# Products of constants in TensorE's order at the norms of a two-block transformer kernel

## The chip, the cores and the metric

The kernel runs on one core of a Trainium2 chip. The metric is the device time of one execution in microseconds (us). Three runs of the kernel before gave 3358.14, 3357.20 and 3356.77 us, median 3357.2.

## The reference

One sequence of 512 tokens of width 1024 goes through three transformer layers: two of a first block (the first one also carries 256 context tokens) and one of a second block. Each layer is

```python
x = x + 0.5 * m[2] * swiglu(modulate(x, g0, m[0], m[1]), wi1, wo1)
x = x + m[5] * mixer(modulate(x, g1, m[3], m[4]))
x = x + 0.5 * m[8] * swiglu(modulate(x, g2, m[6], m[7]), wi2, wo2)
```

with `modulate(z, g, shift, scale) = rmsnorm(z, g) * (1.0 + scale) + shift`, where `rmsnorm` divides each token by the root of the mean of its squares. The mixer is window attention beside gated linear attention in the first layer, a pooling mixer in the second, and mLSTM beside dilated attention in the third. After the first block, and again at the end, stands `rmsnorm(x, final_g)`. All inputs are float32. So there are eleven norms on the way: three in each layer, one between the blocks, one at the end.

## The kernel before

The state `XT` lies in SBUF with features on the 128 partitions, in eight blocks `k` of 128 features by 512 tokens (768 with the context). A program of `Step` objects is written in one order; each engine then walks that order and emits its own part of every step, so the order of the steps is the order of each engine's queue. Each engine waits by semaphores.

Dense products keep fp32 accuracy by splitting: a weight and an activation each become a rounded high part (`WH`, `HH`) and a low rest (`WL`, `HL`), and `dense` (L197 to L202) issues three products of 512 columns for each block of 128 by 128. Small products, the norms' sums and spreads among them, take plain fp32 operands. The program issues such a call once, and the trace shows it as two MATMUL instructions: 48 calls at L489 stand there as 96.

A norm has these parts, on four engines:

- While the stage before still adds its results to `XT`, ScalarE squares each block and VectorE adds the squares into `SA` (`Sums`, L418).
- `RstdSum` (L474): TensorE waits for the last addition, then sums `SA` over the partitions, one call of 128 columns for each 128 tokens (L489, four calls, six with the context). VectorE and ScalarE then compute the factor, one over the root, in six short operations (`Newton`, L463 to L471).
- `RstdSpread` (L501): TensorE waits for the factor, then spreads it over all partitions into banks 4 and 5 (L513, as many calls).
- `NormSplit` (L543): VectorE multiplies a block by the factor (L581), ScalarE rounds it with the shift into `HH` (L562), VectorE takes the rest into `HL` (L570). TensorE's first dense product waits for the first block's `HL`. In `Up` of the first chunk (`c == 0`) the 48 products go block by block, six for each of the eight blocks.

`rstd_of` (L2941) adds the sum and the spread. It is called by `norm_split` for every feed-forward and for both attention mixers, by `mixer_pool`, and by `final_norm` (L2995), that is at ten of the eleven norms; the first norm, in `start`, has its own order. `final_norm` ends in `FinalNorm` (L588), which multiplies the eight blocks of `XT` on VectorE (L612); between the two blocks it also collects the next norm's squares, and TensorE has nothing to do in it. `P.K` holds constants: its columns 0 to 127 are ones, and 128 to 255, `P.ID`, are the identity. Bank 3 belongs to the first products of a feed-forward and is empty at these places.

Of the kernel before, what the change touches and what calls it, by code (L numbers as in the profile page):

```python
# [17 lines left out]
T = 512  # L18
# [28 lines left out]
NONE = Tok(None, 0)  # L47


class Sig:  # L50


    def __init__(self, sem):
        self.sem, self.n = sem, 0
# [18 lines left out]
class Step:  # L73
# [3 lines left out]
    def tensor(self, pe):  # L77
        pass
# [4 lines left out]
    def vector(self, dve):  # L83
        pass
# [364 lines left out]
class Newton:  # L449
# [11 lines left out]
    def vector(self, dve, R, V, ss, width):  # L461
        dve.wait_ge(*self.ready)
        dve.e.tensor_scalar(V, ss, 1.0 / width, EPS, ALU.mult, ALU.add).then_inc(self.v.sem, 1)  # L463
        dve.wait_ge(*self.root)
        dve.e.reciprocal(R, R).then_inc(self.inv.sem, 1)
        dve.wait_ge(*self.inv)
        dve.e.scalar_tensor_tensor(V, V, -0.5, R, ALU.mult, ALU.mult).then_inc(self.half.sem, 1)
        dve.wait_ge(*self.half)
        dve.e.tensor_tensor(V, V, R, ALU.mult).then_inc(self.prod.sem, 1)
        dve.wait_ge(*self.prod)  # L470
        dve.e.scalar_tensor_tensor(R, V, 1.5, R, ALU.add, ALU.mult).then_inc(self.done.sem, 1)  # L471


class RstdSum(Step):  # L474
# [2291 lines left out]
class Program:  # L2766
# [171 lines left out]
            self.add(ModDone(self, 0, 1, 2, dot))  # L2938
            return [muled, dot]

    def rstd_of(self, nq):  # L2941
        self.add(RstdSum(self, nq))
        self.add(RstdSpread(self, nq))

    def norm_tiles(self, ctx, two):
        sb = lambda n, s: self.sb(ctx, self.name(n), s, F32R)
        return H(sb("HH", [128, 8, T]), sb("HL", [128, 8, T]), sb("HC", [128, 8, 2 * TC]) if two else None)
# [45 lines left out]
        self.spread = step.done  # L2993

    def final_norm(self, gname, again):  # L2995
        self.rstd_of(T // 128)
        self.add(FinalNorm(self, gname, Sums(self, T) if again else None))

# [700 lines left out]
```

## Time and profile before

| | |
|---|---|
| median of three runs | 3357.2 us |
| profiled execution | 3361.52 us, of which 3359.7 us span |
| TensorE busy, matmul | 3120.8 us, 93% |
| VectorE busy | 1905.1 us, 57% |
| ScalarE busy | 1024.9 us, 31% |
| mean granted TensorE clock | 0.955 of full speed |

One execution was recorded. Times in its rows are microseconds from the start of the span unless marked ns. PE is TensorE's matmul, PEld its weight load, DVE VectorE, ACT ScalarE. A matmul's duration contains the way through the array, so that matmuls overlap; what one costs in a stream is the distance of its start to the next one's. PEclk is the granted clock as a share of 2.4 GHz; it has two levels here, 1.00 and 0.50 (1.2 GHz).

### The profile page before, as it was taken

Reading aid. Unit: us, or ns where it says so; the run is one execution under the profiler, and the core shown is the slowest. Engines: PE = TensorE matmul, PEld = TensorE weight load, DVE = VectorE, ACT = ScalarE, POOL = GpSimd, SP = SyncE. Lnnn points to the kernel's source line nnn. Section 1 sums busy time; section 2 is a strip of 40 time slices with the busy share of each in tenths; the row PEclk is TensorE's granted clock in tenths of the full one; section 3 lists DMA queues with packets and bytes.
Section 4 is the critical chain, followed back from the end, with each engine's and each line's share of the span. In section 5 each row is a group of like instructions: output and inputs, shape, how many; then the busy total and the mean of one; then the engine's idle time right before and its main releaser. Section 6 shows DMA issues by size and latency. Waiting matters only on the chain.

```text
span 3359.7 us, 36404 instructions
## 1 busy us (share of the span) xinstructions
PE 3120.8 (93%) x14707; PEld 2504.8 (75%) x14718; DVE 1905.1 (57%) x2717; ACT 1024.9 (31%) x1476; POOL 28.0 (1%) x30
## 2 busy tenths in 40 slices
PE   4999999898889999999997999979998998899998
PEld 3788888786667888778876788768887764577886
DVE  6876555635555544566656654566665555654344
ACT  2322222335433222322224222332223434432222
POOL 2000000000000000000000000000000000000000
PEclk6999999998999999999997999989999999799999
DMA  5433332110023433255531443225551210122321
GB/s 192 132 128 129 125 113 97 52 63 16 1 95 112 161 126 121 82 188 187 189 114 63 157 144 132 94 82 188 194 194 54 82 57 1 49 90 94 100 95 50
DMA packets 101794, 364.98 MB, mean 109 GB/s; under 512 B 11198, under 2 KB 12494, under 8 KB 101372
## 3 DMA queue, kind: packets, MB, share of 16 engines
q1 hardware_dynamic: 97644, 351.65, 31.2%
q10 hardware_dynamic: 2944, 6.29, 0.5%
q0 software_dynamic: 1040, 4.71, 0.4%
q8 instruction: 118, 1.93, 0.2%
q14 instruction: 48, 0.39, 0.0%
HBM read 360.51 MB, written 2.10 MB: 108 GB/s over the span
## 4 chain that ended last, share of the span: by engine, by line
PE 85%; DVE 9%; ACT 3%; issue 1%; DMA 1%; ACTq 0%; POOL 0%; DVEq 0%; SPq 0%; POOLq 0%
PE ps L197 24%; PE ps L199 24%; PE ps L198 24%; PE ps L201 4%; PE ps L202 2%; DVE WL L189 1%; DVE DUMP L310 1%; DMA STG<-in_w_modt 1%; ACT WH L184 1%; DVE RAW L1278 1%; PE ps L513 1%; PE ps L2563 1%; PE ps L2323 1%; PE ps L2633 0%; PE ps L2663 0%
## 5 line engine op out<-in xcount | busy, mean ns | idle before, releaser
L197 PE MATMUL ps<-HH,WH 128*128 128x512 f32 x2464 | 979.9, 398 | 35.0 <-DVE HL L570 28.4
L199 PE MATMUL ps<-HH,WL 128*128 128x512 f32 x2464 | 967.6, 393 | 0.0
L198 PE MATMUL ps<-HL,WH 128*128 128x512 f32 x2464 | 967.5, 393 | 0.0
L184 ACT ACTIVATE WH<-RAW 128x1024 fp32r<-128x1024 f32 x456 | 456.9, 1047 | 554.7 <-PE ps L199 410.1
L189 DVE TENSOR_TENSOR WL<-RAW,WH 128x1024 fp32r<-128x1024 f32 x456 | 538.5, 1221 | 85.6 <-ACT WH L184 85.4
L197 PEld LDWEIGHTS ps<-HH,WH 128*128 128x128 f32 x2464 | 468.0, 190 | 142.7 <-issue 40.8
L198 PEld LDWEIGHTS ps<-HL,WH 128*128 128x128 f32 x2464 | 468.3, 190 | 100.2 <-issue 4.6
L199 PEld LDWEIGHTS ps<-HH,WL 128*128 128x128 f32 x2464 | 467.5, 190 | 99.8
L821 DVE SCALAR_TENSOR_TENSOR XT<-ps,DER,XT 128x512 f32<-128x512 f32 x512 | 342.8, 682 | 272.3 <-PE ps L199 257.8
L197 PE MATMUL ps<-GH,WH 128*128 128x512 f32 x1056 | 414.2, 392 | 19.1 <-DVE XT L821 14.3
L762 DVE TENSOR_TENSOR S<-S,ps 128x512 f32<-128x512 f32 x132 | 90.8, 688 | 568.1 <-PE ps L199 568.1
L198 PE MATMUL ps<-GL,WH 128*128 128x512 f32 x1056 | 411.9, 390 | 0.0
L199 PE MATMUL ps<-GH,WL 128*128 128x512 f32 x1056 | 411.6, 390 | 0.0
L744 ACT ACTIVATE GH<-S 128x512 fp32r<-128x512 f32 x132 | 83.4, 632 | 670.6 <-DVE S L762 670.6
L310 DVE SCALAR_TENSOR_TENSOR DUMP<-RAW,CC 128x1024 bf16<-128x1024 f32 x200 | 244.4, 1222 | 11.6 <-DVE DUMP L310 0.5
L197 PEld LDWEIGHTS ps<-GH,WH 128*128 128x128 f32 x1056 | 198.8, 188 | 67.1 <-DVE XT L821 18.6
L199 PEld LDWEIGHTS ps<-GH,WL 128*128 128x128 f32 x1056 | 198.8, 188 | 42.2
L198 PEld LDWEIGHTS ps<-GL,WH 128*128 128x128 f32 x1056 | 198.9, 188 | 38.5
L740 ACT ACTIVATE S<-ps 128x512 f32<-128x512 f32 x132 | 79.0, 598 | 293.2 <-PE ps L199 293.2
L201 PE MATMUL ps<-HC,WH 128*128 128x512 f32 x424 | 151.8, 398 | 0.0
L764 DVE TENSOR_TENSOR GL<-S,GH 128x512 fp32r<-128x512 f32 x132 | 91.4, 692 | 100.3 <-ACT GH L744 100.3
L202 PE MATMUL ps<-HC,WL 128*128 128x256 f32 x424 | 118.8, 280 | 0.0
(355 smaller groups left out, 2424.9 us busy)
## 6 DMA issues: line engine op xcount, KB each, us to landing
RAW<-in_w_modt SPq DMA_DIRECT2D x200, 512.0 KB, 4.5
RAW<-in_ffn_wi SPq DMA_DIRECT2D x176, 512.0 KB, 4.4
RAW<-in_ffn_wo SPq DMA_DIRECT2D x88, 512.0 KB, 4.7
RAW<-in_w_gu SPq DMA_DIRECT2D x88, 512.0 KB, 4.3
RAW<-in_w_in SPq DMA_DIRECT2D x44, 512.0 KB, 3.7
RAW<-in_w_down SPq DMA_DIRECT2D x44, 512.0 KB, 4.5
RAW<-in_w_out SPq DMA_DIRECT2D x16, 512.0 KB, 4.5
MU<-in_w_mod SPq DMA_DIRECT2D x8, 384.0 KB, 9.0
```

The lines of the kernel that those rows point to most:

```text
L184: act.e.activation(u.hi, u.ld.view, ACT.Copy).then_inc(u.hi_done.sem, 1)
L189: dve.e.tensor_tensor(u.lo, u.ld.view, u.hi.bitcast(F32), ALU.subtract).then_inc(u.lo_done.sem, 1)
L197: pe.e.matmul(out, wh, x[0], start=first, stop=False)
L198: pe.e.matmul(out, wh, x[1], start=False, stop=False)
L199: m = pe.e.matmul(out, wl, x[0], start=False, stop=last)
L201: pe.e.matmul(out, wh, x, start=first, stop=True, skip_group_check=not first)
L202: m = pe.e.matmul(out[:, 0:TC], wl, x[:, 0:TC], start=False, stop=True, skip_group_check=True)
L310: dve.e.scalar_tensor_tensor(self.dump, self.view, 1.0, tile[:, :], ALU.mult, ALU.mult, accum_out=self.P.DOT[:, self.row % 2, j, self.f:se ...
L744: act.e.activation(gh, s, ACT.Copy).then_inc(self.hi[n].sem, 1)
L762: dve.e.tensor_tensor(s, s, F.SX[:, :] if n else out, ALU.mult).then_inc(self.mul[n].sem, 1)
L764: dve.e.tensor_tensor(gl, s, gh.bitcast(F32), ALU.subtract).then_inc(self.lo[n].sem, 1)
L821: dve.e.scalar_tensor_tensor(x, o, P.mod_g(F.mi, d, j), x, ALU.mult, ALU.add).then_inc(self.evac[d, n][i].sem, 1)
```

## The change

A new step `Busy(n)` puts `n` fp32 calls into TensorE's order, each with the identity as the stationary operand and 256 columns of the constants moving, written to bank 3, where nobody reads them. At nine norms eight calls stand ahead of the sums, twelve between the sums and the spread, and ten behind the spread. At the last norm only the eight stand. In the final norm between the blocks, a further `Busy(4)` follows each of the first seven blocks, with a wait for that block. Nothing else changes: no other engine gets a new instruction.

```diff
--- before.py
+++ after.py
@@ -469,6 +469,19 @@
         dve.e.tensor_tensor(V, V, R, ALU.mult).then_inc(self.prod.sem, 1)
         dve.wait_ge(*self.prod)
         dve.e.scalar_tensor_tensor(R, V, 1.5, R, ALU.add, ALU.mult).then_inc(self.done.sem, 1)
+
+
+class Busy(Step):
+
+
+    def __init__(self, P, n, after=NONE):
+        self.P, self.n, self.after = P, n, after
+
+    def tensor(self, pe):
+        P = self.P
+        pe.wait_ge(*self.after)
+        for _ in range(self.n):
+            pe.e.matmul(P.banks[3][:, 0:256], P.ID, P.K[:, 0:256], start=True, stop=True)
 
 
 class RstdSum(Step):
@@ -2938,9 +2951,15 @@
             self.add(ModDone(self, 0, 1, 2, dot))
             return [muled, dot]
 
-    def rstd_of(self, nq):
+    def rstd_of(self, nq, last=False):
+        self.add(Busy(self, 8))
         self.add(RstdSum(self, nq))
+        if last:
+            self.add(RstdSpread(self, nq))
+            return
+        self.add(Busy(self, 12))
         self.add(RstdSpread(self, nq))
+        self.add(Busy(self, 10))
 
     def norm_tiles(self, ctx, two):
         sb = lambda n, s: self.sb(ctx, self.name(n), s, F32R)
@@ -2993,8 +3012,11 @@
         self.spread = step.done
 
     def final_norm(self, gname, again):
-        self.rstd_of(T // 128)
-        self.add(FinalNorm(self, gname, Sums(self, T) if again else None))
+        self.rstd_of(T // 128, last=not again)
+        final = self.add(FinalNorm(self, gname, Sums(self, T) if again else None))
+        if again:
+            for k in range(7):
+                self.add(Busy(self, 4, final.done[k]))
```

## Rows read from the trace of the kernel before

**Rows 1.** The page: the chain that ended last, by engine.

```profile
PE 85%; DVE 9%; ACT 3%; issue 1%; DMA 1%; ACTq 0%; POOL 0%; DVEq 0%; SPq 0%; POOLq 0%
```

**Rows 2.** TensorE by line: count, busy us, mean ns, idle before.

```profile
L197 PE MATMUL ps<-HH,WH 128*128 128x512 f32 x2464 | 979.9, 398 | 35.0 <-DVE HL L570 28.4 <-DVE WL L189 5.1 <-ACT S L740 1.2
...
L489 PE MATMUL ps<-SA,K 128*6 128x128 f32 x96 | 16.9, 338 | 60.6 <-DVE SA L418 31.6 <-POOL SA L446 29.0
```

**Rows 3.** Timeline, TensorE at one norm: start us, us, line, tiles, count, idle before.

```profile
1002.23 0.39 PE L199 MATMUL ps<-MH,WL 128*128 128x512 f32 x1
1004.86 1.04 PE L489 MATMUL ps<-SA,K 128*6 128x128 f32 x8 [2.24 <-DVE SA L418]
1008.52 2.07 PE L513 MATMUL ps<-R,SEL 6*128 6x128 f32 x8 [2.63 <-DVE R L471]
1013.13 0.76 PE L197 MATMUL ps<-HH,WH 128*128 128x512 f32 x1 [2.54 <-DVE HL L570]
```

**Rows 4.** Stretches around that norm: busy by engine, then PEclk, DMA share, GB/s.

```profile
1002.62:1005.62 3.00, 0.76 (x7) 0.62 (x8) 2.04 (x3) 2.12 (x3) 0.00 (x0) 1.00 0.81 295
1006.00:1016.00 10.00, 4.94 (x15) 4.09 (x16) 7.06 (x13) 3.09 (x5) 0.00 (x0) 0.50 0.00 0
```

**Rows 5.** Timeline, TensorE in the pool mixer: products of 256 and of 140 columns.

```profile
1777.41 0.28 PE L1108 MATMUL ps<-WPH,HH 128*128 128x256 f32 x1
1777.53 0.28 PE L1109 MATMUL ps<-WPH,HL 128*128 128x256 f32 x1
...
1779.56 2.07 PE L1146 MATMUL ps<-BAND,Z 128*128 128x136 f32 x16
```

**Rows 6.** Timeline, TensorE near the start: fp32 products of 512 columns.

```profile
12.05 3.76 PE L266 MATMUL ps<-CC,K 128*128 128x512 f32 x4
15.60 2.05 PE L266 MATMUL ps<-CX,K 128*128 128x512 f32 x4
```

**Rows 7.** Timeline, TensorE: dense products at full clock, then one fp32 call.

```profile
1016.40 0.39 PE L199 MATMUL ps<-HH,WL 128*128 128x512 f32 x1
...
1025.24 0.39 PE L199 MATMUL ps<-HH,WL 128*128 128x512 f32 x1
1025.47 1.02 PE L266 MATMUL ps<-CC,K 128*128 128x512 f32 x2
...
1026.56 0.40 PE L198 MATMUL ps<-HL,WH 128*128 128x512 f32 x1
```

**Rows 8.** Stretches from a norm's first product to the 49th, three of six.

```profile
1013.13:1025.47 12.34, 12.34 (x48) 10.11 (x49) 12.03 (x16) 8.01 (x10) 0.00 (x0) 0.88 0.00 0
1390.82:1403.72 12.90, 12.90 (x49) 10.49 (x50) 12.51 (x16) 8.01 (x10) 0.00 (x0) 0.84 0.04 4
...
2205.27:2218.82 13.55, 13.55 (x48) 10.99 (x49) 12.50 (x16) 8.00 (x10) 0.00 (x0) 0.80 0.06 13
```

**Rows 9.** Timeline, TensorE at the norm ahead of the hybrid mixer.

```profile
2575.88 1.86 PE L489 MATMUL ps<-SA,K 128*6 128x128 f32 x8 [2.24 <-DVE SA L418]
```

**Rows 10.** Timeline, TensorE at the norm of the first mixer, with six column blocks.

```profile
642.19 0.28 PE L202 MATMUL ps<-GC,WL 128*128 128x256 f32 x1
645.49 1.48 PE L489 MATMUL ps<-SA,K 128*6 128x128 f32 x12 [3.02 <-DVE SA L418]
650.64 2.79 PE L513 MATMUL ps<-R,SEL 6*128 6x128 f32 x12 [3.67 <-DVE R L471]
655.97 0.76 PE L197 MATMUL ps<-HH,WH 128*128 128x512 f32 x1 [2.53 <-DVE HL L570]
```

**Rows 11.** Timeline, TensorE: the first product of the pool mixer.

```profile
1770.99 0.55 PE L1108 MATMUL ps<-WPH,HH 128*128 128x256 f32 x1 [4.48 <-DVE HL L570]
```

**Rows 12.** Timeline, TensorE from the final norm between the blocks on.

```profile
2184.11 2.07 PE L513 MATMUL ps<-R,SEL 6*128 6x128 f32 x8 [2.63 <-DVE R L471]
2196.17 1.87 PE L489 MATMUL ps<-SA,K 128*6 128x128 f32 x8 [9.98 <-DVE SA L418]
...
2205.27 0.77 PE L197 MATMUL ps<-HH,WH 128*128 128x512 f32 x1 [2.53 <-DVE HL L570]
```

## The prediction

> **What bounds the kernel now.** I read the chain of work that ended last first: 85% of it is TensorE [rows 1], and the table beside it says that TensorE is busy for 93% of the span. So whatever is put into TensorE's order is free only where TensorE waits, and only for as long as it waits. Next come TensorE's groups by line, for the waits: the norms' sums stood after 60.6 us of idle time, the first products behind a norm after most of 28.4 us [rows 2]. Then one norm in order of time [rows 3]: the last dense product starts at 1002.23, the sums at 1004.86, the spread at 1008.52, the first dense product at 1013.13. The three gaps are 2.24, 2.63 and 2.54 us. Last, the granted clock there [rows 4]: it is 1.00 after the last product, and 0.50 (1.2 GHz) from before 1006.0 to 1016.0, with TensorE busy for only 4.94 of these 10 us. The spread and the first dense products run at half speed. That is what can be won: not the waits, which belong to VectorE and ScalarE, but the slow work between them.
>
> **The price of one added call.** No call of this very form is in the trace. The program's fp32 call is two instructions in the trace, as the count at L489 shows. Between dense products at full clock, one such call of 512 columns stands from 1025.47 to 1026.56 together with one dense product [rows 7]. Dense products are 0.227 apart (39 steps from 1016.40 to 1025.24), so the call took 0.86 us, and 256 columns would take 0.43. From below, sixteen fp32 instructions of about 140 columns, weights of 128 by 128 as here, take 2.07 us with the last one's way through the array, about 0.12 each [rows 5], so the weight load does not show even there. From above, a dense product of 512 columns in one pass takes 0.227, twice that is 0.453. I take 0.43 us, because [rows 7] is the same operation at twice the width, with 0.427 and 0.453 as bounds; at the lower clock it is 0.86. Eight calls are then 3.44 us, twelve 5.16, ten 4.30, four 1.72. The first three are each longer than the gap that they stand in.
>
> Dense products of 256 columns are only 0.12 apart [rows 5]; by that pace a call of two instructions would be 0.24 us. The Trainium skill says much the same (TensorE: Matmul & The Clock Gate, Back-to-back issue gap: a matmul of 256 columns every 262 cycles at full clock, 0.11 us). The skill also says that true fp32 takes four passes (FP8 and Floating Point Precision, TensorE Precision Notes), with which the 0.86 us agrees. By the first figure the change would win time, about the sum of the first rival below, which is worked out from the row.
>
> **One ordinary norm, step by step** (at 1002) [rows 3].
> - Ahead of the sums: the last product holds TensorE to 1002.46, eight calls to 1005.90, against 1004.86: **+1.04**.
> - Ahead of the spread: the four calls of the sums hold TensorE for about 0.88 (eight instructions, 0.11 apart, from their 1.04 us), then twelve calls: the spread starts 6.04 after the sums, where the factor let it start after 3.66: **+2.38**. The factor itself is ready on time; the spread is queued behind the calls.
> - Behind the spread: at full clock it occupies 0.88 too, then ten calls, so the first product comes 5.18 after the spread's start. Before it was 4.61 (2.07 of slow spread, then 2.54 of the first block on VectorE and ScalarE, whose HL the first product waits for). **+0.57**. The 1.0 us that the fast spread wins is inside this.
> - So the first dense product comes 3.99 us late. Then it is repaid: the 48 products of the first chunk took 12.34 us at a mean clock of 0.88 [rows 8]; at full clock they are 48 x 0.227 = 10.88. Before, they would have had to wait for VectorE's blocks at that pace; now the blocks are ahead, since TensorE comes 3 us after them. **-1.46**. Net **+2.5**.
>
> **The other norms.** The stretch of 48 products exists at six norms, from 12.34 to 13.55 us, together 78.13, so 12.85 us are won back in all six [rows 8].
> - The norm at 1382: the same 3.99, less 2.02: +2.0.
> - At 2576 and 2968 the sums themselves were slow, 1.86 us instead of 1.04 [rows 9], because the clock fell ahead of them. The calls keep it up: 3.99 - 0.83 = 3.16 late, less 2.28 and 2.23: +0.9 each.
> - At 1801, behind the pool mixer, the clock is low already when the eight calls begin, and they cost up to 0.86 each until it rises. I estimate +1.6 ahead of the sums (1.0 to 3.5), then as at 2576: +1.5.
> - At 645, with six column blocks, the last product is a short one and the wait is 3.02 [rows 10]: 642.31 + 3.44 = 645.75, +0.26; 12 x 0.11 + 5.16 = 6.48 against 5.15, +1.33; 1.32 + 4.30 = 5.62 against 5.33, +0.29. 1.9 late. The slow clock lasts there to 661, 5.1 us from the first product, of which 2.4 come back: -0.5.
> - Ahead of the pool mixer, TensorE waits 4.48 us behind the spread, since VectorE first splits the pool weights [rows 11]. The lateness is 2.0 at the first product and its slow products run six us; I take 0, between -0.8 and +0.8.
> - The last norm has only the eight calls: +1.04, and perhaps a faster spread, whose cold 2.07 would be 1.05: +0.5.
>
> **The norm between the blocks** is the largest term [rows 12]. Before, TensorE has one wait of 9.98 us there while VectorE scales eight blocks. Now 10 + 7 x 4 + 8 = 46 calls stand between the spread and the next sums, 19.8 us, and the waits on blocks do not matter, as VectorE's pace is about 1.3 us a block and four calls take 1.72. The first spread starts at 2184.11 + 1.04 + 2.38 = 2187.53; with 0.88 + 19.78 the next sums start at 2208.19, against 2196.17: +12.0. Then +6.04 and +5.18: the first product at 2219.41 against 2205.27, 14.1 late. 2.67 come back: **+11.5**.
>
> **The sum:** 2.5 + 2.0 + 0.9 + 0.9 + 1.5 - 0.5 + 0 + 0.5 + 11.5 = **+19.3 us**. On the profiled execution of 3361.5 that is 3380.8; the median of the runs lies 4.3 lower, so 3357.2 + 19.3 = **3376.5**. The stages behind the norms are TensorE's own, so nothing there takes the lateness back. With 0.427 and 0.453 for a call (some 270 calls lie on the path) the sum is 18.5 to 25, the estimated terms add 3 either way.
>
> **The rivals.**
> 1. *A call costs 0.24 us*, two dense instructions of 256 columns. Then 1.92 and 2.40 us fit into the waits of 2.4 and 3.57 (the last with the spread), 2.88 misses by 0.1, and four calls (0.96) fit between the blocks. Each norm wins the 1.0 of the spread and some 1.2 to 2.4 behind it, the four slow sums 0.8 each: -24, **3333**. Against it stands [rows 7]. The sign turns at about 0.34 us a call: there eight calls cost +0.3, twelve +1.3, ten win 0.35, and repayment covers the rest.
> 2. *The calls do not keep the clock up.* They are made of ones and zeros. Then a call is 0.86 us: eight cost +4.5, twelve with a slow sum and spread +8.1, ten +5.8, nothing is repaid, 18 a norm; with the 46 calls the sum is near +175, **3530**. Against it: products with a diagonal matrix, nearly all zeros, ran four in 3.76 us at the start, and the next four in 2.05 [rows 6]; the clock rose on them.
> 3. *The lateness is taken back later*: TensorE finds weights and banks further ahead than now, which saves it the 5.1 us of waits on `WL` and some at chunk borders [rows 2]. Then +9: **3366**.
>
> **How the numbers follow.** Forecast 0.80, rival 1 0.07, rival 2 0.04, rival 3 0.09. The likeliest gives 3376.5. Its own bounds are 3372 to 3385; to take in rival 3 and an error in the estimated terms I give **3365 to 3389**. A measurement of this kernel can tell about 0.2% (6.7 us) from no change. Faster 0.07 (rival 1), within 0.2% 0.05 (part of rival 3), slower 0.88.
>
> **What would show it.** TensorE's groups get 2 x 306 = 612 instructions at the new line, 0.21 to 0.23 us apart. The waits at L489, L513 and at the first L197 behind a norm vanish from TensorE; the spreads take 1.05 instead of 2.07; the granted clock stays 1.00 through every norm, its mean near 0.99. The sums stand 1.0 us later after the last product, the spread 6.0 after the sums, the first product 5.2 after the spread. Between 2187 and 2208 TensorE is full while VectorE waits. Starts 3.7 us after the sums and a first product 3.6 after the spread would show rival 1; a clock of 0.50 in the new calls rival 2.

## The result and the profile after

The changed kernel takes 3384.6 us (median of four runs, 3379.2 to 3385.1) against 3357.5 us for the kernel before. The ratio is 1.0077, with a 95% interval of 1.0065 to 1.0089, so it is slower by 27 us (22 to 30). The profiled execution has 3385.1 us and a span of 3383.3 us, 23.6 us more than the span before.

The page of the changed kernel: busy time, the granted clock in 40 slices, and the chain that ended last.

```profile
PE 3224.4 (95%) x15330; PEld 2597.4 (77%) x15330; DVE 1904.4 (56%) x2717; ACT 1024.8 (30%) x1476; POOL 27.9 (1%) x30
...
PEclk6999999998999999999999999999999999799999
...
PE 88%; DVE 7%; ACT 3%; issue 1%; DMA 1%; ACTq 0%; DVEq 0%; SPq 0%
```

TensorE is busy 103.6 us more and its share of the chain grew from 85% to 88% [rows 1]. The mean granted clock rose from 0.955 to 0.973. More clock and more time together: what the clock gave is less than what the new calls took.

TensorE's groups by line and shape. The sums are now L502, the spreads L526, the new calls L484.

```profile
L197 PE MATMUL ps<-HH,WH 128*128 128x512 f32 x2464 | 973.6, 395 | 17.6 <-DVE HL L583 10.2 <-DVE WL L189 6.6 <-ACT S L753 0.4
...
L484 PE MATMUL ps<-K 128*128 128x256 f32 x612 | 139.3, 384 | 0.0
...
L526 PE MATMUL ps<-R,SEL 6*128 6x128 f32 x96 | 14.9, 301 | 6.0 <-DVE R L471 6.0
L502 PE MATMUL ps<-SA,K 128*6 128x128 f32 x96 | 13.6, 291 | 29.9 <-POOL SA L446 29.9
```

The waits that the change aimed at are gone. The idle time ahead of the sums was 60.6 us and is 29.9, all of it at the kernel's start; that ahead of the first products fell from 28.4 to 10.2, of which the first norm, which has no new calls, holds nearly everything [rows 2]. The 96 instructions of the spreads take 14.9 us where they took 23.9:

```profile
L513 PE MATMUL ps<-R,SEL 6*128 6x128 f32 x96 | 23.9, 426 | 30.7 <-DVE R L471 30.7
```

One norm in order of time, the one shown as [rows 3].

```profile
1002.44 0.39 PE L199 MATMUL ps<-MH,WL 128*128 128x512 f32 x1
1002.67 3.61 PE L484 MATMUL ps<-K 128*128 128x256 f32 x16
1006.21 1.04 PE L502 MATMUL ps<-SA,K 128*6 128x128 f32 x8
1007.18 5.45 PE L484 MATMUL ps<-K 128*128 128x256 f32 x24
1012.56 1.15 PE L526 MATMUL ps<-R,SEL 6*128 6x128 f32 x8
1013.64 4.58 PE L484 MATMUL ps<-K 128*128 128x256 f32 x20
1017.88 0.58 PE L197 MATMUL ps<-HH,WH 128*128 128x512 f32 x1
```

No row has an idle time any more. Eight calls stand from 1002.67 to 1006.21, 0.44 us each. The sums start 3.77 us behind the last dense product's start instead of 2.63, the spread 6.35 behind the sums instead of 3.66, the first product 5.32 behind the spread instead of 4.61: 4.5 us late.

Four stretches, with PEclk third from the end: the one that was at 0.50 before [rows 4], the first 48 products [rows 8], the stretch in which the calls behind the pool mixer begin (at 1804.03), and the norm between the blocks.

```profile
1006.00:1016.00 10.00, 10.00 (x53) 8.16 (x52) 4.11 (x8) 1.65 (x3) 0.00 (x0) 1.00 0.01 4
1017.88:1028.80 10.92, 10.92 (x50) 9.02 (x49) 10.65 (x14) 7.10 (x9) 0.00 (x0) 1.00 0.00 0
1802.50:1805.75 3.25, 3.25 (x13) 2.89 (x13) 3.25 (x6) 1.60 (x3) 0.00 (x0) 0.50 0.76 255
2187.00:2208.00 21.00, 21.00 (x103) 17.75 (x103) 13.01 (x22) 7.52 (x13) 0.00 (x0) 1.00 0.00 1
```

In the first, TensorE is busy all the time and the clock stays at 1.00 (it was 0.50, with 4.94 of 10 us busy). In the second, the 48 products run at full clock. From the first start to the last they take 10.9 us where they took 12.1; up to the start of the product behind them, as [rows 8] counts, 11.1 instead of 12.34. In the third the clock was low before the calls began, and rose behind 3.25 us of busy TensorE; these eight calls take 4.5 us and not 3.5. In the fourth TensorE is full for 21 us with new calls and one group each of sums and spreads, while VectorE, which has the real work there, is busy for 13.

The norm between the blocks, in the place of [rows 12].

```profile
2195.86 1.15 PE L526 MATMUL ps<-R,SEL 6*128 6x128 f32 x8
2196.95 20.12 PE L484 MATMUL ps<-K 128*128 128x256 f32 x92
2217.00 1.04 PE L502 MATMUL ps<-SA,K 128*6 128x128 f32 x8
...
2223.35 1.15 PE L526 MATMUL ps<-R,SEL 6*128 6x128 f32 x8
...
2228.66 0.58 PE L197 MATMUL ps<-HH,WH 128*128 128x512 f32 x1
```

The span of 23.6 us can be put down place by place, from the last product of one norm to that of the next, each against the same stretch of the kernel before:

| norm near (before) | forecast | measured |
|---|---|---|
| 645 | -0.5 | -0.1 |
| 1005 | +2.5 | +3.3 |
| 1383 | +2.0 | +2.8 |
| 1761, pool mixer | 0 | 0.0 |
| 1801 | +1.5 | +1.7 |
| 2180 and 2196 | +11.5 | +13.0 |
| 2576 | +0.9 | +0.7 |
| 2968 | +0.9 | +1.7 |
| the last | +0.5 | +0.2 |
| ahead of all | 0 | +0.3 |

### The profile page after: what moved, and what is told of

Same layout as the page of the kernel before. It is cut to its first block, busy times and chain, and to the rows that moved or that the text cites. A ratio compares the mean times of both kernels' runs of the same rounds, so it can differ in the third digit from the quotient of the medians.

```text
span 3383.3 us, 37639 instructions
## 1 busy us (share of the span) xinstructions
PE 3224.4 (95%) x15330; PEld 2597.4 (77%) x15330; DVE 1904.4 (56%) x2717; ACT 1024.8 (30%) x1476; POOL 27.9 (1%) x30
## 3 DMA queue, kind: packets, MB, share of 16 engines
q8 instruction: 123, 2.02, 0.2%
## 4 chain that ended last, share of the span: by engine, by line
PE 88%; DVE 7%; ACT 3%; issue 1%; DMA 1%; ACTq 0%; DVEq 0%; SPq 0%
PE ps L197 24%; PE ps L199 23%; PE ps L198 23%; PE ps L484 4%; PE ps L201 4%; PE ps L202 2%; DVE WL L189 1%; DVE DUMP L310 1%; DMA STG<-in_w_modt 1%; ACT WH L184 1%; DVE RAW L1291 1%; PE ps L2576 1%; PE ps L2676 1%; PE ps L2336 1%; PE ps L2646 0%
## 5 line engine op out<-in xcount | busy, mean ns | idle before, releaser
L197 PE MATMUL ps<-HH,WH 128*128 128x512 f32 x2464 | 973.6, 395 | 17.6 <-DVE HL L583 10.2
L484 PE MATMUL ps<-K 128*128 128x256 f32 x612 | 139.3, 384 | 0.0
```

Of the source, the lines that this page charges most:

```text
L197: pe.e.matmul(out, wh, x[0], start=first, stop=False)
L484: pe.e.matmul(P.banks[3][:, 0:256], P.ID, P.K[:, 0:256], start=True, stop=True)
```

## The experiments

The theory: the calls hold TensorE longer than the waits last (the overhang), while the clock that they keep up gives back less. Rivals: the number of calls costs and not their length; the clock needs more than such calls to stay up; one of the four places carries the loss. Kernels of one group below ran on one chip with the kernel before.

### Half the width

```diff
-            pe.e.matmul(P.banks[3][:, 0:256], P.ID, P.K[:, 0:256], start=True, stop=True)
+            pe.e.matmul(P.banks[3][:, 0:128], P.ID, P.K[:, 0:128], start=True, stop=True)
```

> The changed kernel with the same calls in the same places, each 128 columns wide instead of 256. If a call costs its columns (0.44 us now, 0.22 then), eight take 1.8 us, sums plus twelve 3.6, spread plus ten 3.1, four 0.9: all fit into the waits of 2.4, 3.66, 3.6 and 1.26 us. Then no sum and no spread is late, every spread takes 1.15 instead of 2.07, the first products run at full clock: 3333 us (3329 to 3340), 24 below the kernel before. Rival, the lateness comes from the number of instructions or of weight loads and not from their length: 3384, as the changed kernel. Second rival, the clock needs wider products than these to stay up: spreads of 2.07 and a time near 3357.

Measured: 3340.2 us (3336.1 to 3341.3), ratio 0.9948, interval 0.9933 to 0.9963. The same norm in its timeline:

```profile
1002.23 1.95 PE L484 MATMUL ps<-K 128*128 128x128 f32 x16
1004.63 1.04 PE L502 MATMUL ps<-SA,K 128*6 128x128 f32 x8 [0.46 <-DVE SA L418]
1005.60 2.94 PE L484 MATMUL ps<-K 128*128 128x128 f32 x24
1008.48 1.15 PE L526 MATMUL ps<-R,SEL 6*128 6x128 f32 x8
1009.56 2.50 PE L484 MATMUL ps<-K 128*128 128x128 f32 x20
1012.16 0.47 PE L197 MATMUL ps<-HH,WH 128*128 128x512 f32 x1
```

The same number of instructions and of weight loads now fits: 0.46 us of wait are left ahead of the sums, the spread comes 3.85 behind them (3.66 before), and the first product 7.53 behind them, 0.7 sooner than before (8.27). A call is 0.24 us (2.88 for twelve), a little over half of 0.44. So the length of the calls decides, not their number. The spread takes 1.15 us, and the 48 products behind it 11.3 us from the first start to the last instead of 12.1. They do not reach the changed kernel's 10.9, because they begin earlier and the blocks set their pace: VectorE finishes one every 1.45 us, six products take 1.36, and ahead of each block the weight load waits 0.22 us for ScalarE's `HH`. The time is 17 us below the kernel before, 7 less of a gain than the 24 expected. Two causes can be read off: at each of the six norms with 48 such products [rows 8] the stretch is 0.6 us longer than at full clock alone, and at eight norms the twelve calls still overhang by 0.19. That is about 5 of the 7 us, as an estimate from these rows.

### Fewer calls

```diff
-        self.add(Busy(self, 8))
+        self.add(Busy(self, 5))
...
-        self.add(Busy(self, 12))
+        self.add(Busy(self, 6))
...
-        self.add(Busy(self, 10))
+        self.add(Busy(self, 5))
...
-                self.add(Busy(self, 4, final.done[k]))
+                self.add(Busy(self, 2, final.done[k]))
```

> The changed kernel with calls of 256 columns but fewer of them, by the measured 0.44 us each: 5 ahead of the sums (2.2 us in 2.4), 6 behind them (0.97 + 2.7 in 3.66), 5 behind the spread (0.97 + 2.2 in 3.6), 2 for each block of the norm between the blocks (0.9 in 1.26). If the changed kernel is slower only by the overhang of its calls: 3333 us (3329 to 3340), with the clock at 1.00 through the norms. If short gaps between calls and work already let the clock fall: spreads of 2.07 again, and about 3357.

Measured: 3335.2 us (3329.7 to 3338.4), ratio 0.9934, interval 0.9919 to 0.9949; a second group gave 3334.7 us (3329.6 to 3340.7), ratio 0.9933. The timeline of the same norm:

```profile
1001.27 1.04 PE L502 MATMUL ps<-SA,K 128*6 128x128 f32 x8
1002.24 2.86 PE L484 MATMUL ps<-K 128*128 128x256 f32 x12
1005.03 1.15 PE L526 MATMUL ps<-R,SEL 6*128 6x128 f32 x8
1006.11 2.42 PE L484 MATMUL ps<-K 128*128 128x256 f32 x10
1008.72 0.47 PE L197 MATMUL ps<-HH,WH 128*128 128x512 f32 x1 [0.18 <-DVE HL L583]
```

This version beats both kernels: it is 22 us below the one before and 49 below the changed one, with the same idea and fewer calls. Sums to spread 3.76 us (3.66 before, 6.35 changed), spread to first product 3.69 (4.61, 5.32).

### Without, and only, the calls between the blocks

```diff
-        if again:
-            for k in range(7):
-                self.add(Busy(self, 4, final.done[k]))
```

> The changed kernel without the seven groups of four calls in the norm between the blocks; the rest is kept. If these hold up the next sums by TensorE's queue: VectorE's chain decides there again, the sums start 9.9 us after the spread's end instead of 20, so 10 us less than the changed kernel, 3374 to 3375. If VectorE or the clock set that stretch: no difference, 3384.

Measured: 3373.6 us (3371.6 to 3375.5), ratio to the kernel before 1.0052 (1.0035 to 1.0069). That is 11 us less than the changed kernel. The expectation from the queue was 10. In the traces the sums come 10.0 us earlier, of which 1.7 are lost again as told below, so 8.3 of the 11 belong to this place; the rest lies in stretches that the edit does not touch. The norm between the blocks there:

```profile
2194.28 8.04 PE L484 MATMUL ps<-K 128*128 128x256 f32 x36
2204.33 1.04 PE L502 MATMUL ps<-SA,K 128*6 128x128 f32 x8 [2.02 <-DVE SA L418]
2205.30 7.13 PE L484 MATMUL ps<-K 128*128 128x256 f32 x24
```

The sums wait 2.02 us for VectorE again, so VectorE's chain decides; they start 10.1 us behind the first of these rows, where the changed kernel has 20.1 (2217.00 - 2196.95). The third row is a side effect: twelve calls of 5.45 us elsewhere took 7.13 here, since the clock fell to 0.50 from 2206.0 to 2209.25, behind that wait.

The complement keeps these seven groups and drops the eight, twelve and ten calls everywhere.

> The kernel before with nothing but the seven groups of four calls in the norm between the blocks. The clock is low when they begin (0.86 us a call) and rises after some 3.5 us; the 28 calls last 14 us from the first block, the next sums come 4.9 us late, run fast (-0.8), and their spread and the first products may run fast too (-1.0, -2.7). Net +0.5 to +4: 3358 to 3361. If the calls did not raise the clock: 28 x 0.86 = 24 us, sums 15 us late, 3372.

Measured: 3363.4 us (3359.6 to 3366.5), ratio 1.0018 (1.0009 to 1.0027), a little above the range given.

```profile
2188.64 15.19 PE L484 MATMUL ps<-K 128*128 128x256 f32 x56 [0.84 <-DVE XT L625]
2203.76 1.04 PE L502 MATMUL ps<-SA,K 128*6 128x128 f32 x8
```

The 28 calls take 15.1 us, where full clock would make them 12.4, since the clock rises only at 2194.5, 5.9 us after their start. The sums come 24.3 us behind the last dense product, against 18.4 before: 6.0 late instead of the 4.9 expected. The late rise of the clock is what I had priced too low. Up to the next norm the place costs 3.6 us net in this trace; the rest of the loss lies where nothing was changed. At the norm near 1005, for one, the 48 products take 13.6 us from the first start to the last, where the kernel before has 12.1 with the same instructions. So where the clock is not held, a single norm differs by up to 1.5 us from one trace to another, and what follows is read over the six norms with 48 such products.

### Each of the three groups alone

The kernel before with one line of `rstd_of` added, in three kernels:

```diff
+        self.add(Busy(self, 8))     # only_sums
         self.add(RstdSum(self, nq))
+        self.add(Busy(self, 12))    # only_factor
         self.add(RstdSpread(self, nq))
+        self.add(Busy(self, 10))    # only_block
```

> The kernel before with only the eight calls ahead of the sums, at the ten norms. They overhang by 1.1 us (0.3 at the first, up to 3 behind the pool mixer), but the sums are never slow again, and the clock, kept up later, may still be up for the spread 2.7 us after the sums. If the lateness adds up place by place and the clock pays it back: 3360 (3354 to 3365). If the eight calls alone account for the loss of the changed kernel: 3370 or more.

Measured: 3358.5 us (3357.5 to 3362.6), ratio 1.0005 (0.9996 to 1.0014): no difference that can be told.

```profile
1003.38 1.04 PE L502 MATMUL ps<-SA,K 128*6 128x128 f32 x8
1007.05 1.15 PE L526 MATMUL ps<-R,SEL 6*128 6x128 f32 x8 [2.63 <-DVE R L471]
1010.74 0.77 PE L197 MATMUL ps<-HH,WH 128*128 128x512 f32 x1 [2.54 <-DVE HL L583]
```

The eight overhang as in the changed kernel, and the spread is fast without any call ahead of it (1.15). But the clock falls at 1009.5, in the wait behind the spread, and the 48 products run partly at half speed again: 13.4 us from the first start to the last. Over the six norms they take 77.5 us, where the kernel before has 76.8 and the changed kernel 65.3. So these calls win nothing in the products. Their overhang of 1.1 us at a norm stands against 0.9 us from the fast spread and 0.8 from the sums where these were slow, which comes to nearly nothing.

> The kernel before with only the twelve calls behind the sums, at nine norms. The spread comes 2.7 us late, runs fast (-0.9), and the first products run fast (-1.3 to -2.1): about +0.3 at a norm with fast sums, +1.5 more where the clock was low already when the twelve begin. Place by place: 3365 (3358 to 3371). If the twelve are the main loss, as their overhang is the largest of the three, this run lies above the two beside it.

Measured: 3380.2 us (3379.1 to 3380.8), ratio 1.0069 (1.0052 to 1.0086). This is 15 above the middle of what I expected, the largest miss of the study.

```profile
1004.22 1.18 PE L502 MATMUL ps<-SA,K 128*6 128x128 f32 x8 [2.24 <-DVE SA L418]
1005.33 6.94 PE L484 MATMUL ps<-K 128*128 128x256 f32 x24
1012.20 1.15 PE L526 MATMUL ps<-R,SEL 6*128 6x128 f32 x8
1015.89 0.77 PE L197 MATMUL ps<-HH,WH 128*128 128x512 f32 x1 [2.53 <-DVE HL L583]
```

```profile
1005.25:1008.25 3.00, 3.00 (x8) 2.36 (x8) 2.06 (x5) 0.31 (x1) 0.00 (x0) 0.50 0.02 8
1008.50:1015.00 6.50, 4.86 (x26) 3.94 (x24) 1.42 (x3) 0.76 (x2) 0.00 (x0) 1.00 0.00 0
1015.25:1022.00 6.75, 6.11 (x14) 4.81 (x15) 6.57 (x10) 3.21 (x5) 0.00 (x0) 0.50 0.00 0
```

The first group of rows is its timeline, the second shows three stretches of it. Two things had been left out. The clock falls around the sums, since the wait ahead of them has no calls, and the twelve calls begin at 0.50 and take 6.94 us instead of 5.45. Then it rises, and falls again behind the 2.53 us of wait ahead of the first product, for the whole of 1015.25 to 1022. The 48 products take 13.6 us. Over the six norms they take 79.1 us against 76.8 before, where I had expected a gain of 1.3 to 2.1 at each. At this norm the overhang at full clock is 2.7 us, the low clock in the calls adds 1.6, the fast spread gives back 0.9. The twelve are the worst of the three alone, as the second theory said, but the miss comes from the clock and not from the overhang.

> The kernel before with only the ten calls behind the spread, at nine norms. The clock is down when they begin (0.88 us a call) and rises 3 to 4 us after the spread's start; the first product comes 2.6 to 4 us late, and the 48 products behind it run fast (-2.1). Place by place: 3365 (3358 to 3372). If calls at a low clock did not raise it: first products 5.8 late and nothing won, above 3395.

Measured: 3373.2 us (3366.9 to 3373.8), ratio 1.0045 (1.0030 to 1.0060), 1 us above the range given. The trace is that of the fastest of the four executions, 6 us below their median.

```profile
1009.64 2.07 PE L526 MATMUL ps<-R,SEL 6*128 6x128 f32 x8 [2.62 <-DVE R L471]
1011.64 7.12 PE L484 MATMUL ps<-K 128*128 128x256 f32 x20
1018.41 0.59 PE L197 MATMUL ps<-HH,WH 128*128 128x512 f32 x1
```

The spread is slow (2.07), the ten calls begin at the low clock and take 6.77 us up to the first product, against 4.24 in the changed kernel. The first product comes 8.8 us behind the spread's start, 4.2 late, and the 48 products then run fast (10.9 us), as expected.

The three alone add 1.4, 23.1 and 16.1 us, 40.6 together; all three in one kernel (the run without the calls between the blocks) add 16.5. So the losses of the three groups do not add up, although the expectations assumed it: a group is paid at full clock only if the group ahead of it has kept the clock.

### The third group in the fitted kernel

```diff
-        self.add(Busy(self, 5))     # behind RstdSpread
```

> The kernel of the run called fit (5, 6, 5 and 2 calls) without the five behind the spread. TensorE is then idle for 2.5 us ahead of the first product, with the clock up. If the clock needs the third group: it is down for some of the first products, 1 to 2 us at a norm, 3342 to 3350. If a gap of 2.5 us behind busy work is short enough: 3335, as fit.

Measured: 3348.2 us (3345.7 to 3349.5), ratio 0.9972 (0.9961 to 0.9982). Three stretches of its norm near 1010; the first product starts at 1012.66.

```profile
1009.00:1014.00 5.00, 2.47 (x15) 1.98 (x14) 3.57 (x6) 2.00 (x3) 0.00 (x0) 1.00 0.00 0
1014.25:1017.45 3.20, 3.20 (x9) 2.52 (x9) 3.13 (x5) 1.45 (x2) 0.00 (x0) 0.50 0.00 0
1017.75:1024.00 6.25, 6.25 (x30) 5.13 (x29) 6.05 (x8) 4.79 (x6) 0.00 (x0) 1.00 0.00 0
```

Behind the wait of 2.5 us the clock is lost. It falls to 0.50 only at about 1014.2, when the products have been running for 1.5 us, and stays there for 3.2 us. The same is seen at all six norms: the 48 products take 12.2 to 13.6 us, and 11.3 in the fitted kernel. Thirteen of the 22 us that the fitted kernel wins hang on five calls that TensorE spends while VectorE prepares the first block. The kernel with this one wait left open is still 9 us below the kernel before.

### Two more places mended

In the fitted kernel, 7 and 8 calls instead of 5 and 6 at the norm with six column blocks, and five calls in the pool mixer's last wait:

```diff
-        self.add(Busy(self, 5))
+        self.add(Busy(self, 5 if nq < 6 else 7))
...
-        self.add(Busy(self, 6))
+        self.add(Busy(self, 6 if nq < 6 else 8))
...
+            self.add(Busy(self, 5, copies[3].done))
             mean(3)
```

> The kernel of the run called fit once more, beside the next one on the same chip: 3335 us (3330 to 3340).

> The kernel fit with two places mended where its trace still shows the lower clock: 7 and 8 calls instead of 5 and 6 at the norm with six column blocks (gaps of 0.87 and 1.03 us there, after which five calls took 3.80 us instead of 2.2), and five calls in the pool mixer's last wait of 2.78 us (behind which five calls took 3.82). If a mean gap of about 1 us is enough to lose the clock and filling it keeps it: 1.9 and 2.5 us less, some 4 below fit, 3331. If the clock falls in the pool mixer from its earlier waits in any case: 2 less, 3333.

Measured: 3334.7 us for the fitted kernel and 3334.7 us (3328.3 to 3339.3) for the mended one. In the mended kernel's trace the clock stays at 1.00 through both places. Against the first trace of the fitted kernel the stretches are shorter by 1.2 us (last product to first product, 12.6 against 13.8) and 1.0 us (last product ahead of the pool mixer to the first one behind it, 49.1 against 50.1). But the second trace of the fitted kernel, with 5 and 6 calls, has 12.7 us at the first place, with the clock at 1.00 there too, and 49.5 at the second. So at the first place a gain by the added calls is not shown. At the second the clock was at 0.50 in both traces of the fitted kernel and is at 1.00 in this one, which is worth 0.4 to 1.0 us. That is below what these runs tell apart, as a single kernel's runs spread over 11.

## Why the prediction was right

The forecast was +19.3 us, 3376.5, in a range of 3365 to 3389. The measured 3384.6 lies in it, 8 above the forecast and at the edge of the narrower bounds of the likeliest case, 3372 to 3385. The sign and the mechanism are those forecast. By its steps:

- **The price of a call** was 0.43 us; it is 0.44 (3.54 us for eight, 5.38 for twelve; ten take 4.24 up to the first product, which is then 0.41 ahead of the next one and not 0.23). The step from the fp32 call of 512 columns [rows 7] carried the whole result. The half-width run shows that the price goes nearly by the columns: 0.24 for 128.
- **The overhangs** of an ordinary norm were +1.04, +2.38 and +0.57; they are +1.14, +2.69 and +0.71. The term that was mis-sized is the second: the four calls of the sums hold TensorE for 0.97 us and not 0.88, and the twelve calls take 5.38 and not 5.16. Over nine such groups that is 2.8 of the 4.3 us by which the span grew beyond the forecast.
- **The repayment** was set at 1.46 us at this norm, from 12.34 to 10.88 us; counted in the same way the stretch takes 11.11, so 1.23 came back. Over the six norms 11.5 us came back and not 12.85. Most of the difference is the 0.18 us by which the last call holds up the second product. That the products would no longer wait for VectorE's blocks was right.
- **The norm between the blocks** was +11.5 and is +13.0, with 46 calls of 0.44 us. Taking out the 28 gave 11 us back, 8.3 of them in this place, so it was rightly the largest term.
- **The clock** stays at 1.00 through the norms, with the one exception named: behind the pool mixer it is low when the eight begin. The sums there start 6.28 us behind the last group of products instead of 5.17, so 1.1 late, less than my 1.6. Wrong was the mean, forecast near 0.99 and measured 0.973. The norms hardly lower it any more, but stretches without new calls do, which the forecast had not counted: it is 0.53 between 20 and 85 us, 0.85 between 795 and 945 and 0.83 between 2775 and 2945, both inside mixers.
- **Rival 1**, a call of 0.24 us, was wrong in its price but right in its conclusion: with calls of just 0.24 us, the half-width run, the kernel is faster. Its time of 3333 was too low by 7.
- **Rival 2**, a clock that the calls do not hold, is excluded by the stretches at 1.00.
- **Rival 3**, lateness taken back later, did not happen: at 1005 the first product is 4.5 us late, 1.2 come back in the 48 products, and the next norm begins 3.3 later. At 1383 and 2968 the stage behind gives nothing back either; only at 2576 a further 1.0 us returns. The waits on `WL` are 6.6 us, not fewer than the 5.1 of before.

The medians moved by 27.2 us and the two profiled executions by 23.6. The profiled execution of the kernel before lay 4.3 above its median, that of the changed kernel 0.5 above. So of the 8 us between forecast and measured median, 4.3 are errors of the terms above, and the rest is that the two traced executions do not lie alike to their medians. What that consists of was not looked into; it is within the interval of the ratio.

## What to carry to other kernels

Work that only keeps TensorE's clock up has to be cut to the wait that it fills, with the price of the call taken at its full width and type: here 256 fp32 columns are 0.44 us, and with 8, 12 and 10 calls the kernel lost 27 us, with 5, 6 and 5 it won 22. Fill every wait of a row: one gap of 2.5 us left open cost 13 of the 22 us, and a group placed behind an open gap itself runs in part at half speed (6.94 us for twelve calls instead of 5.45). A single group alone won nothing in any of the three runs. Sum the overhang over every place, since in a queue in order a call that outlasts the wait delays everything behind it.

## What the runs showed of the hardware

- Products with the identity and with ones and zeros hold the granted clock at 1.00, as dense products do: for 20 us between the blocks TensorE had nothing else.
- The clock need not fall in the gap itself. Behind a wait of 2.5 us it fell when products had already been running for 1.5 us, and stayed at 0.50 for 3.2 us; behind a wait of 2.0 us it fell 1.7 us after TensorE had begun again, and stayed there for 3.3 us. In the kernel with the eight calls alone it fell inside the second of two waits.
- An fp32 call is two instructions in the trace, with 0.22 us each for 256 columns and 0.12 for 128 at full clock, weights of 128 by 128 loaded anew each time. The time nearly follows the columns, so the load adds little if anything.
